# Attention: values weighed per head in 64 columns of the array, and softmax sums divided out at the end

## The reference

```python
def forgetting_attention(q, k, v, log_f):          # "fox"
    Ft = jnp.cumsum(log_f, axis=1).transpose(0, 2, 1)
    for start in range(0, S, Q_BLOCK):
        s = einsum('bqhd,bkhd->bhqk', q[:, start:end], k[:, :end]) * scale
        s = s + Ft[:, :, start:end, None] - Ft[:, :, None, :end]
        s = jnp.where(tk <= tq, s, -jnp.inf)
        p = jax.nn.softmax(s, axis=-1)
        outs.append(einsum('bhqk,bkhd->bqhd', p, v[:, :end]))

def dsa_attention(q, k, v, qi, ki, wi):            # one key/value head, 256 keys kept per query
    ...                                            # score by an indexer, idx = top_k(score, 256)
        p = jax.nn.softmax(s over the chosen keys)
        outs.append(einsum('bhqk,bqkd->bqhd', p, vg))
```

## Time and profile before

| what | value |
|---|---|
| median of 3 runs | 3101.01 us (3096.8 to 3103.73) |
| the profiled execution | 3098.0 us, of which the span of the profile is 3095.9 us |
| `attend` in the profile | from about 1853 to 2197 us |
| granted TensorE clock, whole span | 0.934 of full speed |

### The profile page before, as it was taken

How to read it: one execution, slowest core, us unless ns; L and a number is a source line. 1 busy time by engine, 2 the same in 40 slices (tenths; PEclk the granted TensorE clock), 3 DMA queues, 4 the chain that set the end, 5 groups by cost and what they waited for, 6 DMA issues and landing times.

```text
span 3095.9 us, 35168 instructions
## 1 busy us (share of the span) xinstructions
PE 2754.6 (89%) x12924; PEld 2207.4 (71%) x12924; DVE 2152.0 (70%) x2892; ACT 1280.4 (41%) x2069; POOL 774.9 (25%) x385
## 2 busy tenths in 40 slices
PE   6999989979588869969979996989899489999998
PEld 3788767755365658858767875777788478888887
DVE  5589865526689944854634898973555479999997
ACT  3233321110166631223224214666532067777775
POOL 1432310000111100000210006555200035566664
PEclk9999999988798889989989998999999689999999
DMA  6222347633454452326543247441232289999996
GB/s 224 77 70 84 104 148 239 204 126 124 158 184 169 176 229 68 102 56 153 105 116 83 99 112 135 110 121 25 89 123 97 116 310 381 381 383 384 388 381 222
DMA packets 236294, 530.82 MB, mean 171 GB/s; under 512 B 30742, under 2 KB 147590, under 8 KB 219859
## 3 DMA queue, kind: packets, MB, share of 16 engines
q1 hardware_dynamic: 173058, 435.96, 40.2%
q0 software_dynamic: 33680, 58.97, 7.8%
q10 hardware_dynamic: 29376, 33.56, 3.1%
HBM read 450.74 MB, written 95.48 MB: 176 GB/s over the span
## 4 chain that ended last, share of the span: by engine, by line
PE 51%; DVE 6%; POOL 2%; ACT 2%; DMA 2%; issue 1%; SPq 1%; DVEq 0%; ACTq 0%; POOLq 0%
PE banks L143 47%; PE banks L153 4%; DVE a_P L2163 1%; DVE c_rows L1518 1%; POOL a_P L2187 1%; ACT a_PT L2206 1%; DVE m_w_low L1621 0%; DVE e_low L2666 0%; POOL a_R L1551 0%; DMA i_q<-iqT 0%; DVE a_R L1556 0%; ACT m_w_low L1614 0%; DMA p_low_raw<-in_w_out 0%; DMA odsaT<-a_o 0%; ACT e_high L2660 0%
## 5 line engine op out<-in xcount | busy, mean ns | idle before, releaser
L2666 DVE TENSOR_TENSOR e_low<-e_raw,e_high 128x4096 fp32r<-128x4096 f32 x99 | 437.9, 4425 | 64.1 <-ACT e_high L2660 64.1
L143 PE MATMUL banks<-m_w_low,p_high 128*128 128x512 f32 (+1 forms) x1248 | 381.0, 389 | 13.3 <-DVE m_w_low L1621 13.3
L2660 ACT ACTIVATE e_high<-e_raw 128x4096 fp32r<-128x4096 f32 x99 | 359.5, 3633 | 26.9 <-DVE e_g L2615 26.9
L143 PE MATMUL banks<-h_high,w 128*128 128x512 f32 (+1 forms) x1024 | 297.9, 373 | 9.1 <-POOL w L373 4.4
L505 DVE SCALAR_TENSOR_TENSOR acc<-img,taps,acc 128x1024 f32<-128x1024 f32 x160 | 259.8, 1625 | 61.6 <-ACT acc L483 56.6
L143 PEld LDWEIGHTS banks<-m_w_low,p_high 128*128 128x128 f32 x1248 | 234.3, 195 | 57.4 <-issue 8.7
L143 PE MATMUL banks<-m_w_low,p_low 128*128 128x512 f32 (+1 forms) x624 | 240.5, 385 | 0.0
L143 PEld LDWEIGHTS banks<-h_high,w 128*128 128x128 f32 x1024 | 186.2, 191 | 49.0 <-POOL w L373 4.9
L143 PE MATMUL banks<-e_high,e_xhigh 128*128 128x512 f32 x528 | 211.5, 401 | 7.1 <-issue 5.5
L143 PE MATMUL banks<-e_high,e_xlow 128*128 128x512 f32 x528 | 208.3, 395 | 0.0
L143 PE MATMUL banks<-e_low,e_xhigh 128*128 128x512 f32 x528 | 207.9, 394 | 0.0
(11 more groups left out here) (495 smaller groups left out, 6245.5 us busy)
## 6 DMA issues: line engine op xcount, KB each, us to landing
e_raw<-in_exp_w SPq DMA_DIRECT2D x99, 2048.0 KB, 13.0
s_sums<-cumT SPq DMA_DIRECT2D x32, 768.0 KB, 4.5
w_raw<-in_w_in SPq DMA_DIRECT2D x20, 1024.0 KB, 6.2
s_X<-xtok SPq DMA_DIRECT2D x19, 1024.0 KB, 7.3
p_raw<-in_w_in SPq DMA_DIRECT2D x18, 1024.0 KB, 7.3
w_raw<-in_ada_w SPq DMA_DIRECT2D x12, 1024.0 KB, 5.4
mod_w<-in_ada_w SPq DMA_DIRECT2D x12, 1024.0 KB, 6.9
w_raw<-in_w_ada SPq DMA_DIRECT2D x10, 1024.0 KB, 8.1
```

The lines of the kernel that those rows point to most:

```text
L143: last = pe.matmul(out, a, b, start=start and n == 0, stop=stop and n == len(pairs) - 1)
L2660: act.activation(self.high[p % HIGHS][:], self.raw[p % RAWS][:], ACT.Copy).then_inc(*self.high_done.up())
L2666: dve.tensor_tensor(self.low[p % HIGHS][:], self.raw[p % RAWS][:], self.high[p % HIGHS][:].bitcast(F32), ALU.subtract).then_inc(*self.low_ ...
```

## The change

`normed` is gone: the probabilities stay unscaled, and PE's transposes wait for the exponentials alone. `inverses` now writes the reciprocal of each sum 64 times, a 128x128 tile `rc` (two heads, 64 columns each). After the transposes of a pair, PE transposes this tile too, into the next of banks 4 and 5, and ACT copies it to `rows`: it then holds, in the partitions of each head's 64 values, the inverse for each of the 128 queries. `weigh_values` issues for each key block and each head its own matmul: 64 stationary columns (that head's values), 128 moving columns, result in partitions 0 to 63 or 64 to 127 of one 128x128 region. `close` moves from ACT to DVE and multiplies the result by `rows` into `o`, which one DMA stores. It stands one iteration later, for pair p-2, ahead of the transposes and of the reciprocals in the order of the loop.

```diff
-            dve.reciprocal(rc[b][:], sm[b][:]).then_inc(*vec.up())
+            if i >= 3:
+                dve.wait_ge(*inverse_turned.at(i - 2))
+            dve.reciprocal(rc[b][:], over(sm[b][:], 2, HD)).then_inc(*vec.up())
...
-        def normed(i):
-            _, j, _ = pairs[i]
-            L, b = P * (j + 1), i % 3
-            pool.wait_ge(*inverse_done[i])
-            both = prob[b][:, :, 0:L]
-            pool.tensor_tensor(both, both, over(rc[b][:], 2, L), ALU.mult).then_inc(*scaled.up())
...
-            pe.wait_ge(*scale_done[i])
+            pe.wait_ge(*exp_done[i])
...
+            q = j // 2 + 1
+            if turns_free[q % 2]:
+                pe.wait_ge(*turns_free[q % 2])
+            pe.wait_ge(*inverse_done[i])
+            turns(pe, [(core.bank[:, 4 + q % 2, 0:P], rc[b][:].rearrange("p e d -> p (e d)"))], ident).then_inc(*inverse_turned.up())
+            act.wait_ge(*inverse_turned.now())
+            if i >= 2:
+                act.wait_ge(*out_free[i - 2])
+            act.activation(rows[i % 2][:], core.bank[:, 4 + q % 2, 0:P], ACT.Copy).then_inc(*inverse_copied.up())
+            turns_free[q % 2] = inverse_copied.now()
...
-            products(pe, out, [(fv[:, k, P * c:P * c + P] if kind == "fox" else dv[:, k, :, :].rearrange("p a d -> p (a d)"),
-                                PT[z][:, k, :, :].rearrange("p e n -> p (e n)")) for k in range(j + 1)]).then_inc(*summed.up())
+            for k in range(j + 1):
+                for e in range(2):
+                    at = P * c + HD * e
+                    last = pe.matmul(core.bank[HD * e:HD * e + HD, 6 + z, 0:P], fv[:, k, at:at + HD] if kind == "fox" else dv[:, k, :], PT[z][:, k, e, :],
+                                     start=k == 0, stop=k == j)
+            last.then_inc(*summed.up())
...
-            act.activation(o[z][:].rearrange("p e n -> p (e n)"), core.bank[:, 6 + z, 0:256], ACT.Copy).then_inc(*closed.up())
+            dve.tensor_tensor(o[z][:], core.bank[:, 6 + z, 0:P], rows[z][:], ALU.mult).then_inc(*closed.up())
...
-            for e in range(2):
-                sp.dma_start(dram[f"o{kind}T"][P * c + HD * e:P * c + HD * e + HD, at], o[z][HD * e:HD * e + HD, e, :]).then_inc(*stored[z].up())
+            sp.dma_start(dram[f"o{kind}T"][P * c:P * c + P, at], o[z][:]).then_inc(*stored[z].up())
...
+            if 0 <= p - 2:
+                close(p - 2)
             if 0 <= p < N:
                 turn_probs(p)
-            if 0 <= p - 1:
+            if 0 <= p - 1 < N:
                 weigh_values(p - 1)
             if 0 <= p + 1 < N:
-                inverses(p + 1), normed(p + 1)
+                inverses(p + 1)
             if p + 2 < N:
                 maxima(p + 2), exponentials(p + 2)
-            if 0 <= p - 1:
-                close(p - 1)
```

More of the change, by code:

```diff
@@ L2066, in attend @@
         dkk, dkl = (s.sb(f"a_{k}", [2 * HD, SEQ], R32) for k in ("dkk", "dkl"))
-        fv, dv = s.sb("a_fv", [P, NT, 512]), s.sb("a_dv", [P, NT, 2, HD])
+        fv, dv = s.sb("a_fv", [P, NT, 512]), s.sb("a_dv", [P, NT, HD])
         qt = [s.sb(f"a_q{b}", [2 * HD, NAH, P], R32) for b in range(2)]
@@ L2071, in attend @@
         R = [s.sb(f"a_R{b}", [P, SEQ]) for b in range(4)]
-        nm, sm, rc = ([s.sb(f"a_{k}{b}", [P, 2]) for b in range(3)] for k in ("nm", "sm", "rc"))
-        o = [s.sb(f"a_o{b}", [P, 2, P]) for b in range(2)]
+        nm, sm = ([s.sb(f"a_{k}{b}", [P, 2]) for b in range(3)] for k in ("nm", "sm"))
+        rc = [s.sb(f"a_rc{b}", [P, 2, HD]) for b in range(3)]
+        o, rows = ([s.sb(f"a_{k}{b}", [P, P]) for b in range(2)] for k in ("o", "inverse"))
         vec, values_in, keys_in = s.sem("a_vec"), s.pair("a_values_in"), s.dma("a_keys_in")
         fox_in, q_in = ahead.fox_in, s.pair("a_q_in")
-        scored, exped, scaled = (s.sem("a_" + k) for k in ("scored", "exped", "scaled"))
+        scored, exped, inverse_turned, inverse_copied = (s.sem("a_" + k) for k in ("scored", "exped", "inverse_turned", "inverse_copied"))
         turned, copied, summed, closed, stored = *(s.sem("a_" + k) for k in ("turned", "copied", "summed", "closed")), s.pair("a_stored")
@@ L2116, in attend @@
         pairs = [("fox", j, c) for c in range(4) for j in reversed(range(NT))] + [("dsa", j, c) for j in range(NT) for c in range(4)]
-        score_ready, exp_done, inverse_done, scale_done, turn_done, copy_done, sum_done, out_free, max_done = ({} for _ in range(9))
+        score_ready, exp_done, inverse_done, turn_done, copy_done, sum_done, out_free, max_done = ({} for _ in range(8))
         def scores(i):
@@ L2212, in weigh_values @@
             z = i % 2
-            out = core.bank[:, 6 + z, 0:256]
             pe.wait_ge(*copy_done[i])
@@ L2228, in close @@
             z, at = i % 2, slice(P * j, P * j + P)
-            act.wait_ge(*sum_done[i])
+            dve.wait_ge(*sum_done[i])
+            dve.wait_ge(*inverse_copied.at(i + 1))
             if i >= 2:
-                act.wait_ge(*stored[z].at(2 * (i // 2)))
-            act.activation(o[z][:].rearrange("p e n -> p (e n)"), core.bank[:, 6 + z, 0:256], ACT.Copy).then_inc(*closed.up())
+                dve.wait_ge(*stored[z].at(i // 2))
+            dve.tensor_tensor(o[z][:], core.bank[:, 6 + z, 0:P], rows[z][:], ALU.mult).then_inc(*closed.up())
             out_free[i] = closed.now()
             sp.wait_ge(*closed.now())
-            for e in range(2):
-                sp.dma_start(dram[f"o{kind}T"][P * c + HD * e:P * c + HD * e + HD, at], o[z][HD * e:HD * e + HD, e, :]).then_inc(*stored[z].up())
+            sp.dma_start(dram[f"o{kind}T"][P * c:P * c + P, at], o[z][:]).then_inc(*stored[z].up())
             if pairs[i] == ("dsa", TOPK // P - 1, 3):
@@ L2251, in load_rest @@
             return vec.now()
-        for half in range(2):
-            sp.dma_start(dv[:, :, half, :], pv[:, :, C_DV:C_DV + HD]).then_inc(*values_in[1].up())
+        sp.dma_start(dv[:], pv[:, :, C_DV:C_DV + HD]).then_inc(*values_in[1].up())
         ahead.load_gates()
         N = len(pairs)
-        for p in range(-2, N + 1):
+        for p in range(-2, N + 2):
             if p == 1:
```

3 lines of the change are left out of this document (1 added, 2 removed).

## The result

The changed kernel took 3107.0 us in the median of 17 runs (3099.28 to 3110.33), the kernel before 3101.0 in as many (3094.15 to 3104.93). The ratio is 1.0019, with a 95% interval of 1.0011 to 1.0026: 6 us slower. The interval lies above 1, but the difference is about the 0.2% that the prediction took as the least that can be told from no change. The forecast was 3109.2 us. The profiled execution of the changed kernel took 3109.31 us (span 3107.5).

A forecast was written before the change was run, and what follows sets the result against it. DVE was taken to bound fox, a DVE-ACT ring the short pairs, PE the last stretch; 18.0 + 1.0 + 7.5 - 3.3 - 17.0 + 2 = +8.2 us on 3101.0 gave 3109.2 us, range 3090 to 3140.

The forecast's parts named there:

- The values on PE: Values matmuls: the two heads' matmuls run at the same time, saving 0.218 us a block; given 2 chances in 3.
- The first rival: The heads' matmuls don't overlap: last stretch pays 5.6 us instead of gaining 17, +31.8, 3133 us; chance 0.27.
- The reciprocal: On DVE, widened from 2 to 128 columns: 0.88 us, +0.72 us a pair; with `close`, 1.01 us a pair.
- The rival of a cheap reciprocal: Wide reciprocal takes only 0.32 us, DVE pays 0.44 a pair: -16.7, 3084 us; chance 0.13.
- Fox: 24 pairs from 1916 us, DVE leads: pays 24.2 us, less 6.2 us of waits for PE: +18.0.
- POOL's products go, but they stood beside DVE's counts: In fox's 24 pairs: removing POOL's scaling products was priced at nothing.
- The last stretch: 16 pairs of dsa, PE leads: 22.6 us saved by overlap, 5.6 added by transpositions and stalls: net -17.0 us.
- the change of width: PE switching stationary columns for the values, two changes a pair: taken to cost nothing.
- the fourth rival: PE drains at each change of tile, 0.16 us a change: the forecast and 5 us, 3114 us; chance 0.03.
- The stalls before the inverse: Last stretch, PE waits for its bank before the transposed inverse: 0.48 us with seven blocks, 0.26 with eight, none with six.
- Short pairs: 15 pairs, 2032 to 2073 us, paced by a ring of DVE and ACT: +7.5, middle between 0 and 15.
- The clock: PE, busy 65% in fox, is granted a slower clock under a leading DVE: 0 to 8 us, taken as +2.

The follow-up runs named there:

- the first experiment: The changed kernel with the loops over key blocks and heads exchanged in the values, so one head's matmuls all precede the other's: 3121.4 us.
- the narrow kernels: The changed kernel with DVE's reciprocal kept at two columns, widened by two PE matmuls (3076.9 us) or by a POOL copy (3076.8 us).
- the kernel without scaling: The kernel before without POOL's product `normed`, outputs left unscaled and transposes waiting for the exponentials: 3085.3 us, ratio 0.9948.
- the narrow reciprocal: The changed kernel with DVE inverting two columns and PE widening them by two matmuls against the identity: 3076.9 us, ratio 0.993.

## Why the prediction was right, and where it was not

**The values on PE: right, and settled.** The heads overlap: two instructions every 0.109 us, 0.22 us a block against 0.43 before. The saving is 0.213, where the prediction put 0.218, and from the first to the last start of a pair with eight blocks it is 1.70 us, where the prediction put 1.7. The first rival (no overlap, 3133 us) is nearly what the first experiment built, at 3121.4 us. It had the last stretch right (+5.6, and +5.0 measured) and was 12 us too slow mostly in fox: it had 21 us there, the 18.0 discussed below and 3 for PE falling behind, where that kernel lost 11.8.

**The reciprocal: right, a little short.** 0.94 us against 0.88 taken by extending small sizes. The rival of a cheap reciprocal falls; the narrow kernels, where it costs still less, are at 3077 us against its 3084. The Trainium skill ("VectorE: DVE Perf Modes", First, the fixed hardware budget) has the reciprocal repeat its divide eight times; the prediction's estimate from that, 1.07 us and more, is above the 0.94 measured. From one start to the next on DVE in fox the reciprocal takes 0.86 us where two columns took 0.11, and `close` adds 0.21 rather than its length of 0.29: 0.96 us a pair, where the prediction had 1.01.

**Fox: +12.0, not +18.0.** The rate and DVE's lead were right (24 x 0.96 = 23.0; the wait of 6.2 us is gone). The three groups of eight pairs took 42.9, 42.7 and 38.5 us, where the prediction wanted some 45 each. The term that failed is the one that read "POOL's products go, but they stood beside DVE's counts". They stood beside the counts, but the small steps between the counts were held: they take 2.6 us less in this stage once the products are gone, in the kernel without scaling and in the changed one alike. The whole stage, read off DVE's instructions: 23.0 more for reciprocals and `close`, 2.6 less for the small step, 7.2 less idle (10.9 to 3.7, with the 6.2 us for PE in it), and 1.2 less elsewhere, which stays unexplained. That is +12.0. The 5.5 us that the kernel without scaling gained in fox can't be taken off as they are, since 1.7 of them are the same wait for PE. Beside each other in the timeline does not mean free of each other.

**The last stretch: -11.4, not -17.0.** The overlap gives 104 x 0.213 = 22.2 us, nearly as forecast, so 10.8 us stand against it where the prediction had 5.6. The prediction gave a sign for this, that pairs of eight blocks come 1.4 us closer together. The values of two such pairs, before and after:

```profile
2177.48 3.62 PE L143 MATMUL banks<-a_PT,a_dv 128*128 128x256 f32 x16
2183.21 3.62 PE L143 MATMUL banks<-a_PT,a_dv 128*128 128x256 f32 x16
...
2191.37 1.97 PE L2228 MATMUL banks<-a_PT,a_dv 128*64 128x128 f32 x32
2196.21 1.97 PE L2228 MATMUL banks<-a_PT,a_dv 128*64 128x128 f32 x32
```

They came from 5.73 to 4.84 us, 0.89 closer. In the same way the first pairs of five, six and seven blocks came closer by 0.33, 0.78 and 0.41 us, where the terms of the prediction give 0.76, 1.20 and 0.94. Each is 0.4 to 0.5 us short. Most of that is the step that failed, the change of width, put at nothing by the earlier trace rows: it costs 0.34 us a pair by the timelines, 5.4 us. I had priced the same in the fourth rival at 5 us and gave it 0.03, on rows of other matmuls (512 moving columns, another number type), and what it described (0.16 us a change) is what the timelines show (0.17). The stalls before the inverse are 0.1 us longer than priced with seven and with eight blocks (0.58 and 0.36 for 0.48 and 0.26, from the last transposition to the inverse, less one step), 0.8 us in all; 0.06 a pair between the inverse and the values is there with 128 columns too. These make more than the 5.6 us that are missing; the last two pairs and what follows them, which the terms did not price apart, gave some 2 us back.

**Short pairs: +6.0 for +7.5; last masks: -2.4 for -3.3; first eight: -0.2 for +1.0.** Signs and sizes hold but for the last, which is near zero either way. For the short pairs the middle between two far bounds was a choice and not a reading; the narrow reciprocal takes back all of it (38.2 us, against 38.8 before). One sign of being wrong that the prediction named did come here, a wait of DVE in `close` for a store (from 2050.6 to 2117.1 us); how much of the +6.0 it makes was not tried:

```profile
DVE a_o L2241 <- DMA ofoxT<-a_o: 3.9, 1, 3.9
```

**The clock: +2, measured nothing.** PE was granted 0.88 in fox, lower as forecast, but DVE waited 0.2 us for it in all, and the kernel with the heads one after the other, granted 0.96 in fox, took the same 124.0 us there. So the clock cost nothing. The busy share behind the forecast was wrong: PE was busy 106 of 129 us, 82% and not 65%. I had taken the saved time off the busy time, and PE's busy time did not fall with it.

The forecast lay 2.2 us from the median because a gain too large by 5.6 us and a charge too large by 6.0 met. That is luck: the two errors have separate causes, a cost of the change of width and a relief of DVE's small steps, each put at nothing. What it had right is the structure: a gain paid out on PE in the last stretch, and a charge on DVE in fox.

## What to carry to other kernels

A change made of two edits can hide a good one behind a bad one: here the values per head are worth 28 us by themselves and the late scaling with its wide reciprocal costs 34. Price each alone before judging the pair, and on DVE keep a reciprocal at as few columns as there are numbers, then widen it elsewhere. The fastest kernel measured has the values per head and nothing else, 3072.8 us; the full change with the two-column reciprocal is at 3076.9 us, and their ranges of runs overlap (3065.89 to 3075.96, 3074.04 to 3079.78), so these two are close. And when a wait or a product is moved to a less busy engine, read what stands behind it in that engine's queue: twice here the removed time came back as a wait behind ACT's exponentials, of PE when the copy of the inverse moved, and of DVE when `close` went to POOL. Before a cost is put at nothing by a row, look whether the row has the same shape: the one of the earlier trace rows had not.

## What the runs showed of the hardware

- Matmuls of 64 stationary and 128 moving columns in float32 start in twos every 0.109 us when neighbours in the queue use different halves of the columns (0.055 each), and 0.109 apart when they use the same half; over all 128 columns it is 0.112. With all of one half first, about 0.38 us of both halves still overlap where they meet.
- Going from 128 to 64 stationary columns and back costs 0.34 us by the timelines, 0.28 by the stretch, for each pair; between 128 and 48 in the earlier trace rows there was no such gap. What makes the difference (the shape, the number type or the length) was not tried.
- A long POOL product in SBUF holds up a small DVE step with two SBUF operands until it ends: 0.45 us at most beside such a product, instead of 0.16. Three steps beside POOL's DMA issues took up to 0.85, only in kernels that have the product; the cause is open. Once a POOL copy to 128 columns held the step too (0.36 us, in the kernel in which POOL widens).
- DVE's reciprocal takes 7.4 ns a column over 128 columns (944 ns), where a product read from PSUM takes 2.2 (287 ns).
